# The softmax division moved from VectorE into the product that turns the probabilities

## What is computed

```
scores = einsum(q, k_ctx) / sqrt(64)
scores = where(valid, scores + bias, -1e30)
probs  = softmax(concat([scores, sink]))[..., :-1]
out    = einsum(probs, v_ctx)
```

## Time and profile before

| | |
|---|---|
| median of 3 runs | 1810.19 us (1809.73 to 1810.88) |
| profiled execution | 1808.18 us |
| its span, first to last instruction | 1806.1 us |
| mean granted TensorE clock | 0.972 of full speed |
| busy share of the span: PE, DVE, ACT, POOL | 94%, 71%, 38%, 16% |

### The profile page before, as it was taken

The page is one execution under the profiler, slowest core; times in us unless marked ns, Lnnn a source line. Parts: engine busy times, 40 slices in busy tenths (PEclk is TensorE's granted clock), DMA queues, the critical chain, the costliest instruction groups (busy, mean ns, idle before and its releaser), DMA issues.

```text
span 1806.1 us, 20425 instructions
## 1 busy us (share of the span) xinstructions
PE 1706.2 (94%) x7314; PEld 1380.2 (76%) x7314; DVE 1290.5 (71%) x1812; ACT 694.9 (38%) x1120; POOL 296.0 (16%) x292
## 2 busy tenths in 40 slices
PE   7689999999988999999999889999999988999998
PEld 4478888888877888777777668888888866878877
DVE  7988676776644758678877799677667753666786
ACT  4343232232234435446644443223232223534442
POOL 6802221112200000024230001212221120000000
PEclk9889999999999999999899989999999989999999
DMA  7215444354377666121123214444444358776433
GB/s 280 82 43 208 169 145 166 143 181 144 125 270 254 213 217 191 57 80 47 36 76 117 82 64 146 169 154 167 163 152 158 122 181 297 226 234 189 152 121 127
DMA packets 122752, 277.69 MB, mean 154 GB/s; under 512 B 9723, under 2 KB 51356, under 8 KB 113948
## 3 DMA queue, kind: packets, MB, share of 16 engines
q1 hardware_dynamic: 115356, 263.02, 43.1%
q10 hardware_dynamic: 7296, 13.37, 2.1%
HBM read 198.23 MB, written 78.12 MB: 153 GB/s over the span
## 4 chain that ended last, share of the span: by engine, by line
PE 77%; DVE 14%; ACT 4%; issue 2%; DMA 2%; SPq 0%; ACTq 0%; DVEq 0%
PE bank L772 25%; PE bank L773 25%; PE bank L774 25%; DVE qb L1778 1%; DVE hn L1393 1%; DMA d_f<-in_wd 1%; PE bank L994 1%; DVE acc L1381 1%; ACT probs L1317 1%; DVE w_lo L1608 1%; DVE x_sb L1413 1%; DVE probs L1790 1%; DVE dn_lo L1661 1%; DVE h_lo L1425 1%; DVE rstd L1386 1%
## 5 line engine op out<-in xcount | busy, mean ns | idle before, releaser
L731 POOL TENSOR_TENSOR wdr<-wdr 128x256 f32<-128x256 f32 x176 | 165.3, 939 | 775.3 <-DMA wdr<-in_wd 765.0
L1661 DVE TENSOR_TENSOR dn_lo<-d_f,dn_hi 128x1024 fp32r<-128x1024 f32 x154 | 186.1, 1223 | 148.3 <-ACT dn_hi L1143 147.6
L772 PE MATMUL bank<-h_hi,t_hi 128*128 128x512 f32 x704 | 279.1, 396 | 6.4 <-DVE h_lo L1425 6.4
L773 PE MATMUL bank<-h_lo,t_hi 128*128 128x512 f32 x704 | 276.4, 393 | 0.0
L774 PE MATMUL bank<-h_hi,t_lo 128*128 128x512 f32 x704 | 276.0, 392 | 0.0
L772 PE MATMUL bank<-dn_hi 128*128 128x512 f32 x616 | 244.7, 397 | 29.7 <-DVE dn_lo L1661 13.9
L773 PE MATMUL bank<-dn_lo,dn_hi 128*128 128x512 f32 x616 | 242.5, 394 | 0.0
L774 PE MATMUL bank<-dn_hi,dn_lo 128*128 128x512 f32 x616 | 242.2, 393 | 0.0
L1143 ACT ACTIVATE dn_hi<-d_f 128x1024 fp32r<-128x1024 f32 x154 | 160.5, 1057 | 196.8 <-DMA d_f<-in_wd 116.7
L772 PE MATMUL bank<-c_hi,t_hi 128*128 128x512 f32 x528 | 205.4, 389 | 0.0
L773 PE MATMUL bank<-c_lo,t_hi 128*128 128x512 f32 x528 | 205.4, 389 | 0.0
(11 more groups left out here) (165 smaller groups left out, 2600.7 us busy)
## 6 DMA issues: line engine op xcount, KB each, us to landing
raw<-in_gu SPq DMA_DIRECT2D x44, 1024.0 KB, 5.7
actc<-acts SPq DMA_DIRECT2D x22, 1792.0 KB, 6.7
d_f<-actc SPq DMA_DIRECT2D x154, 256.0 KB, 3.0
raw_m<-in_units SPq DMA_DIRECT2D x52, 512.0 KB, 4.1
wdr<-in_wd SPq DMA_DIRECT2D x44, 512.0 KB, 5.4
wdc<-wdr SPq DMA_DIRECT2D x44, 512.0 KB, 3.4
d_f<-wdc SPq DMA_DIRECT2D x88, 256.0 KB, 3.2
d_f<-in_wd SPq DMA_DIRECT2D x66, 256.0 KB, 4.2
```

Of the source, the lines that this page charges most:

```text
L731: pool.tensor_tensor(blocks[to], blocks[one], blocks[two], ALU.add).then_inc(wd_made, 1)
L772: pe.matmul(ps, whi, vhi, start=first, stop=False, skip_group_check=onto)
L773: pe.matmul(ps, whi, vlo, start=False, stop=False, skip_group_check=onto)
L1661: dve.tensor_tensor(dn_lo[slot][:, :], d_f[slot][:, :], plain(dn_hi[slot][:, :]), ALU.subtract).then_inc(dn_split, 1)
```

## The change

Where VectorE multiplied the 128 x 256 probabilities of each head by the reciprocal of their sum, it now multiplies the 128 x 128 identity by it, into a new tile `diag` (four heads, 128 x 128 each, at the place of the tile `rstd0`). TensorE then multiplies the unscaled `probs` block (stationary) by that diagonal (moving), which turns and scales it at once: an ordinary float32 product instead of a transpose. VectorE also gets two waits for `probs_turned` of the unit before: ahead of the biasing, since `probs` is rewritten there, and ahead of the diagonals.

```
+        diag = place("diag", (P, HPK, P), rstd_at[0])
...
                     for kb in ((1,) if u < 2 else (0, 1)):
                         for h in range(HPK):
-                            last = pe.transpose(probsT_bank[kb][:, h * P:(h + 1) * P],
-                                                probs[:, h, kb * P:(kb + 1) * P], ident)
+                            last = pe.matmul(probsT_bank[kb][:, h * P:(h + 1) * P],
+                                             probs[:, h, kb * P:(kb + 1) * P], diag[:, h, :], start=True, stop=True)
...
                     dve.wait_ge(scores_made, u + 1)
+                    if u:
+                        dve.wait_ge(probs_turned, u)
                     for h in range(HPK):
...
                     link(dve.reciprocal(stats[:, RCP, :], stats[:, RCP, :]))
+                    if u:
+                        dve.wait_ge(probs_turned, u)
                     for h in range(HPK):
-                        dve.tensor_scalar(probs[:, h, off:], probs[:, h, off:], stats[:, RCP, h:h + 1], None,
+                        dve.tensor_scalar(diag[:, h, :], ident, stats[:, RCP, h:h + 1], None,
                                           ALU.mult).then_inc(probs_normed, 1)
```

## The result

| | before | after |
|---|---|---|
| median | 1809.84 us (20 runs) | 1813.11 us (20 runs) |
| ratio after to before | | 1.0015, 95% interval 1.0008 to 1.0022 |
| profiled execution, its span | 1808.18, 1806.1 us | 1812.97, 1810.9 us |

By the medians the change costs 3.3 us, by the ratio 2.7 (1.4 to 4.0). The forecast was +2.2 (1812.4 us, range 1807.5 to 1820); "within 0.2%" had a chance of 0.49, "slower" 0.42.

The account below looks back on a forecast made before the run. TensorE and VectorE alternately bound units 1 to 7, TensorE units 8 to 14. Unit 8 at -3.0, then +6.1 less 0.9 hidden, gave +2.2 us on 1810.19: 1812.4 us, range 1807.5 to 1820.

Parts of the forecast that it names:

- What bounds the kernel: Attention units: TensorE and VectorE alternately set the pace in units 1 to 7; TensorE busy 72.9 of 74.1 us from 908.9.
- Price of the product: TensorE, each unit: two records per product against one per transpose, 0.87 us more for eight products, 13.1 us in all.
- B: Rival: weight load not hidden, a product costs more than two short records, 2.1 us a unit; 1826.6 us; chance 0.10.
- C: Rival: the product costs TensorE nothing, running as fast as the transpose; 1804.2 us; chance 0.07.
- the 4x of the Trainium skill: Transpose mode 4x faster for FP32: price 2.6 us a unit, about 1831 us; given 0.02 of B's chance.
- The diagonals: VectorE: four diagonals take 0.88 us where four scalings took 1.14; gain 0.26 us per unit from unit 2 on.
- Unit 4's stall: VectorE's unit 4 scaling of 3.38 us becomes 1.72; TensorE idles 0.3 us instead of 3.10, turning shifts by -0.61.
- The clock: TensorE after unit 4: full clock kept instead of 0.51 over 9.9 us, which wastes 4.9 us.
- the ring: Units as a cycle: scores (TensorE), bias and exponentials (VectorE, ScalarE), scaling (VectorE), turning (TensorE), scores of the next unit.
- Hidden in units 1 and 4 to 7: TensorE's waits there, such as 1.83, 3.10, 0.94 and 2.07 us, hide added work; scores of unit 8 at -3.0.
- Seven units paid: Units 8 to 14: +6.1 us, of which waits and a 0.3 in unit 11 leave unit 15's scores at +2.2.
- The end: Loads behind unit 15's scores, ScalarE's rounding and pv(15) form one chain, all moving by +2.2; 3.6 us wait stays.

Follow-up runs that it names:

- run 7: The new kernel with each of the 120 products made twice: 1829.09 us, ratio 1.0104 to the kernel before; the new kernel itself beside it: 1813.85 us.
- run 1: The product alone: VectorE scales as before, TensorE multiplies by the identity instead of transposing; 1812.15 us against 1810.94 for the kernel before, ratio 1.0007.
- run 4: The kernel before, unchanged, profiled a second time: 1809.21 us, one execution.
- run 3: The kernel before with 16 transposes of the identity as filler in TensorE's wait of unit 4: 1810.19 against 1810.94 us, ratio 0.9999.
- run 5: The kernel before with one weight-unit load put ahead of the two weight-quad loads behind unit 15's scores: 1803.84 against 1810.94 us, ratio 0.9966.
- run 8: GpSimd's fourth pooling input waits for unit 4's scaling: kernel before 1807.07 us; second, new kernel 1813.23 us; kernel before with weight-unit load ahead of quads 1798.72 us.

## Why the prediction was right, step by step

- **What bounds the kernel.** Right: units 1 to 7 alternate, units 8 to 14 are TensorE's. The new kernel's waits of VectorE in all of units 9 to 14, and run 7, show it.
- **Price of the product.** Right in kind (two records for one) and nearly in size: 0.91 us a unit, not 0.87. The row of unit 1's scores carried over from 64 rows to 128. Rivals B and C fall with it, and so does the 4x of the Trainium skill (TensorE: Matmul & The Clock Gate, Terms): by it eight products would take 3.5 us (an estimate, four times the 0.87 of the transposes), and they took 1.78.
- **The diagonals.** 0.88 us, as read from unit 0. Worth nothing by themselves here: the change without them measured +1.2 us (run 1), with them +3.3; the intervals overlap, so I don't call them harmful, but they bring no gain.
- **Unit 4's stall.** Mis-sized: 2.25 us instead of 1.72, so the idle time was 1.00, not 0.3, and turning moved by +0.20 instead of -0.61. It was right to take a value between the bounds, but nothing in the old trace said how GpSimd's rows would lie after a shift of 1 to 2 us.
- **The clock.** The size was right, 5 us. The step that led there was wrong: I read from five waits of one execution that the clock falls after 2.58 us and not after 2.07. Other executions lost it after 1.83 and kept it after 2.40 (run 4), and lost it after 2.02 (run 3). So it was luck that the one profile which I read had its low stretch in unit 4 and that 4.9 us is also the average. What fits all profiles is that the change shortens all three waits of the ring; that this, and not the products, keeps the clock up is not shown.
- **Hidden in units 1 and 4 to 7.** Right: the waits shrank from 1.83, 3.10, 0.94 and 2.07 to 1.38, 1.00, 0.26 and 1.39, and unit 8 began at -2.5 (forecast -3.0). In the new kernel's other two profiles it began at -0.7 and -0.3, since the whole row lay later; and against the two other profiles of the old kernel the shift from unit 2 to unit 8 is -1.6 and -5.5 instead of -3.0.
- **Seven units paid.** 4.7 us, forecast 6.1 less 0.9. The waits of units 9 and 11 vanished whole (1.17 us, not 0.87) and 0.5 is unaccounted for, against 0.3 more for the price. The scores of unit 15 came at +2.2, as forecast, because unit 8 began 0.5 later and the seven units cost 0.5 less. That the figure is met to a tenth is luck: in the new kernel's other two profiles they came at +4.1 and +4.4.
- **The end.** The chain through the loads was right (run 5), its length was not constant: the weight unit took 8.97 us instead of 7.84 to land, and pv(15) came at +3.3. The wait before it was 4.73 us, where I had said 3.6. pv(15) moved by 1.1 to 1.4 us more than the scores of unit 15 in all four profiles that have the product once and the loads in their old order (the changed kernel twice, run 1, run 8's second kernel), and in none of those with transposes: SP's three loads behind the scores take 11.7 to 12.0 us there instead of 10.5 to 10.7. So this microsecond comes with the product, and it is what the forecast of +2.2 lacked in this profile against +3.3 at pv(15). Why the loads take longer I can't say.
- **The profile's own surplus.** Its span is 4.8 us longer, not 3.3; the rest is a low stretch of 3.4 us at 1624 us, far from the change, that the old profile doesn't have.

## What to carry to other kernels

Before moving work from an engine that waits to one that is busy, find the stretch in which the busy engine has no wait left: there each microsecond is paid, elsewhere it may be free. The waits of 2 to 4.5 us on TensorE cost twice here, by themselves and by the low clock that may follow, so taking their cause away was worth more than either side of this change: one load put ahead and one GpSimd input put later gave 12 us, 1798.7 against 1811.4. A profile shows one draw of where the clock falls. Judge by the times of many executions, take their mean clock as a sign of how much low clock there is, and profile the old kernel more than once before reading a shift of 1 or 2 us.

## What was not expected of the hardware

- The same wait in the same kernel is followed by a low clock in one execution and not in the next: unit 1's 1.83 us (kept in the first profile, lost in run 4) and unit 4's 2.40 us (kept in run 4, lost in run 5). The wait before pv(7) was followed by one at 2.02 us (run 3) and not at 2.07 and 2.08 (the kernel before).
- VectorE and GpSimd stretch each other. Four scalings of 1.14 us took 3.38 beside GpSimd's L703 and L690, and GpSimd's L702, 0.62 us at best, took 1.43 (run 8) and 1.74 (run 1) where it met VectorE's splitting of a weight unit (L1608). In run 1 a shift of 1 us turned it round: VectorE's row was back at 1.14 and GpSimd's took the 1.74.
